# Two attention heads stacked per tile, and rotation tables made during an earlier feed-forward part and kept in DRAM

## The chip, the core and the metric

One core of one Trainium2 chip. The metric is the device time of one execution of the whole program in microseconds (us). The engines are TensorE (PE, with its weight loads PEld), VectorE (DVE), ScalarE (ACT), GpSimd (POOL), and SyncE (SP), which only issues transfers.

## What is computed

A stack of blocks over 256 tokens of width 1024, batch 1, all in float32. First two layers, each a gated feed-forward, a hybrid mixer and a second gated feed-forward, each with its norms; then a third block with a mixer of its own kind and a feed-forward:

```python
def first_block(x, ...):
    for l in range(DEPTH):          # DEPTH = 2
        f = swiglu(rms_norm(x, ffn1_pre_g[l]), ffn1_w_gu[l], ffn1_w_down[l])
        x = x + 0.5 * rms_norm(f, ffn1_post_g[l])
        m = hybrid_mixer(rms_norm(x, mix_pre_g[l]), ...)
        x = x + rms_norm(m, mix_post_g[l])
        f = swiglu(rms_norm(x, ffn2_pre_g[l]), ffn2_w_gu[l], ffn2_w_down[l])
        x = x + 0.5 * rms_norm(f, ffn2_post_g[l])
def second_block(x, ...):
    h = rms_norm_2(x, mix_norm_g[0])
    (u, c_b, c_c, c_x, q, k_c, v_c, k_s, v_s, k_w, v_w, nsa_gates, mix_gates) = split_projection(h @ w_in[0])
    y_ssm = s5_mixer(u, lam_re, lam_im, b_re, b_im, c_re, c_im, d, log_dt, w_glu)
    y_conv = short_conv_mixer(c_x, c_b, c_c, conv_w, conv_w_out)
    y_attn = nsa_mixer(q, k_c, v_c, k_s, v_s, k_w, v_w, nsa_gates, ...)
    ...                             # gates, w_out, then a last feed-forward
```

Two parts of the third mixer matter here. `s5_mixer` is a diagonal complex state-space recurrence, `lam_bar = exp(lam * exp(log_dt))`, for 32 groups of 64 states. `nsa_mixer` is attention with 8 query heads of width 64 on 2 key heads, with compressed, selected and window keys.

## The kernel before, in words

Every weight matrix is cut into chunks of 128 x 1024 float32 (512 KB), which SP streams into a ring of six slots `raw`. Each chunk is split in two: ACT rounds it to `whi` (`split_hi`, L465), DVE subtracts to get the rest `wlo` (`split_lo`, L472), and PE makes each product in three matmuls (L486 to L488, or L773 and L774 in the feed-forward). A slot is free for the split again once PE has consumed the chunk, so ACT and DVE run at most six chunks ahead of PE.

**The feed-forward** (`ffn_pe`, `ffn_act`, `ffn_dve`) has 22 hidden tiles. PE's order for tile j is gate(j), up(j), down(j-2); the last four down chunks come at the end (`held`) and need the hidden values of tiles 18 to 21. DVE's order for one tile is fixed in `tile`: sum the gate halves (L890), scale (L892), wait for the `wlo` split of one chunk (L472), sum the up halves (L895), multiply (L898), round (L902), subtract (L904), and split two more chunks. ACT's order is silu (L851), then three `whi` splits. The DVE split in the middle waits for the first of these three, which stands behind the silu, which waits for L892. Gate(j) needs the bank that tile j-2 has drained. In all layers tiles 2 to 5 and 18 to 21 are written out, the middle ones are a hardware loop.

**The third mixer** (`mix2_pe`, `mix2_act`, `mix2_dve`, `mix2_pool`) has an order written out by hand. Names are kept in the lists `BANKED2`, `JOBS2`, `BY_ACT2` and `BY_DVE2`, which give each product its PSUM bank and each wait its number. First come projections. Then q and k are transposed per head (L1480, L1487) into `qT` [64, 8, 256] and `kT` [64, 4, 256]; the compressed keys likewise (L1492), and the compressed scores are made per head (`cs0`, `cs1`, L1497). Then 16 rounds r, head h = r // 2 and token tile t = r % 2. PE's round is: scores of the two branches (L1509) with a mask added by a matmul (L1510), the state-space inputs `bu`, the transposes of the round before (L1548), one more streamed projection, values (L1574), and after each second round the state-space outputs (L1538). DVE takes the maximum of the scores (L2128), rotates the inputs by a cosine and sine table (L2137, L2138, L2143, L2144) and scans them (L2148); ACT makes the exponentials (L1823); POOL rotates back (L1918, L1919).

The scores of round r+1 use the same bank as those of round r, so PE waits there until ACT has read them, and ACT waits for DVE's maximum. The first maximum also stands behind DVE's work on `cs0` and `cs1` (L2076 to L2087), from which `pct` (L1556) is made.

The rotation tables have one [128, 2, 2, 256] piece per head, eight in all, made in two buffers (`table` and a part of `par`) one or two heads ahead: `turns` (ACT, L1661 and L1664), `fraction` (DVE, L1938 and L1939), `tables` (ACT, L1674 to L1679, sines, which need another function table of ACT than the exponentials). The coefficients `s5p` are made by small DVE operations on [128, 16] (L1979 to L1987 and L2033 to L2053), and POOL turns the output weights by them once `coef_ready` is set (L1901 to L1911).

Of the kernel before, what the change touches and what calls it, by code (L numbers as in the profile page):

```python
# [43 lines left out]
MIX2_CHUNKS = 90  # L44
HELD = 4
# [19 lines left out]
D_ROUNDS = D_MIXED + 16  # L65
CHANNELS = [f"cv{s}" for s in range(12)] + [f"e{j}" for j in range(len(EARLY))]
# [63 lines left out]
class Place:  # L130
# [17 lines left out]
    def later(self, rounds):  # L148
# [19 lines left out]
           "cv3", "hidt0", "hidt1", "cv4", "cmp0", "cmp1", "cv5", "qt00", "qt01", "qt10", "qt11", "kt0", "kt1", "cv6", "kct", "cs0", "cs1", "cv7"])  # L168
# [38 lines left out]
def block_program(nc, stream, x_in, pf_a, pf_b, pm, pm2, out):  # L207
    ctx = ExitStack()
    with ctx:
# [82 lines left out]
        qT = m1("qT", [HD, 8, S])  # L292
        kT = m1("kT", [HD, 4, S])
        blocks_scope = ExitStack()
        xchi, xclo = [blocks_scope.enter_context(nc.sbuf_tensor(name, [P, 2, 16, 16], F32R)) for name in ("xchi", "xclo")]
        blocks_scope.close()
        otok = m1("otok", [P, T, 512])
        hidT = m1("hidT", [P, 2, 16])
        kcn = m1("kcn", [16, HD])
        kcT = m1("kcT", [HD, 16])  # L300
# [10 lines left out]
        frac = m1("frac", [P, 2, S])  # L311
# [133 lines left out]
        consts2 = sem("consts2")  # L445

# [392 lines left out]
        def ffn_act(act, n, q, place, following):  # L839
# [25 lines left out]
            with act.Fori(0, 4) as i:  # L865
                for u in range(4):
                    j = 2 + u
                    tile(n * (FT - 2) + i * 4 + (u + 1), j, place.later(i * 2), range(3 * j + 3, 3 * j + 6))
            for j in range(18, FT - 1):
                tile(n * (FT - 2) + j - 1, j, place, range(3 * j + 3, 3 * j + 6))  # L870
            tile(n * (FT - 2) + FT - 2, FT - 1, place, [])
# [3 lines left out]
        def ffn_dve(dve, n, q, place, following):  # L875
# [41 lines left out]
            for j in range(2, 6):  # L917
                tile(n * FT + j, n * (FT - 2) + j - 2, j, place, gate_of(j), range(3 * j + 3, 3 * j + 6), free=down_of(j - 4) if j >= 4 else None)
            with dve.Fori(0, 3) as i:
                for u in range(4):  # L920
                    j = 6 + u
                    tile(n * FT + i * 4 + j, n * (FT - 2) + i * 4 + (j - 2), j, place.later(i * 2), gate_of(j), range(3 * j + 3, 3 * j + 6), free=down_of(j - 4))
            for j in range(18, FT):
                split = range(3 * j + 3, 3 * j + 6) if j < FT - 1 else []
                tile(n * FT + j, n * (FT - 2) + j - 2, j, place, gate_of(j), split, free=down_of(j - 4))
# [452 lines left out]
        def mix2_pe(pe, q, r, place, turns):  # L1378
# [95 lines left out]
            for t in range(T):  # L1474
                for b in range(2):
                    name = f"qt{t}{b}"
                    begin2(pe, name)
                    for a in range(4):
                        h = 4 * b + a
                        m = nc.tensor.transpose(bank2(name, slice(a * P, (a + 1) * P))[0:HD], xn[:, t, h * HD:(h + 1) * HD], ident[:, :])  # L1480
                    done(name, m)
            qn_ready.wait(pe, 2 * T)
            for t in range(T):
                name = f"kt{t}"
                begin2(pe, name)
                for a in range(4):
                    m = nc.tensor.transpose(bank2(name, slice(a * P, (a + 1) * P))[0:HD], xn[:, t, 512 + a * HD:512 + (a + 1) * HD], ident[:, :])  # L1487
                done(name, m)
# [1074 lines left out]
```

## Time and profile before

| | us |
|---|---|
| three runs | 1459.5, 1462.04, 1461.91 (median 1461.91) |
| the profiled execution | 1459.69 |
| its span in the trace | 1457.6 |
| PE busy | 1441.8 (99%) |
| DVE busy | 1145.0 (79%) |
| ACT busy | 766.8 (53%) |
| POOL busy | 143.6 (10%) |
| feed-forward two of layer two | about 773 to 950 |
| third mixer | about 951 to 1270, its rounds 1047 to 1167 |

The table reads as a kernel in which one engine is nearly always occupied. Busy PE time is modelled from the starts of pipelined matmuls, so 99% does not say that no time is lost there: a matmul at half clock is as busy as one at full clock. The granted clock has the mean 0.996.

### The profile page before, as it was taken

What the parts mean: (1) busy time and instruction counts of PE and PEld (TensorE: products, weight loads), DVE (VectorE), ACT (ScalarE), POOL (GpSimd) and SP (SyncE); (2) the same over time, 40 slices, a digit from 0 to 9 for tenths busy, and PEclk for the clock granted to TensorE, in tenths of its full rate; (3) what the DMA queues carried; (4) which work ended last, traced back from release to release, by engine and by line L of the source; (5) the groups of instructions that cost most, each with busy time, mean ns of one, the idle gap of its engine ahead of it and who ended that gap; (6) DMA issues with size and microseconds to landing.
All of it is one profiled execution on the core that took longest, in us unless ns stands there. A gap on an engine that the chain in (4) does not pass through costs nothing.

```text
span 1457.6 us, 24445 instructions
## 1 busy us (share of the span) xinstructions
PE 1441.8 (99%) x8561; PEld 1257.9 (86%) x8561; DVE 1145.0 (79%) x1831; ACT 766.8 (53%) x1253; POOL 143.6 (10%) x140
## 2 busy tenths in 40 slices
PE   8999999999999999999999999999999999999999
PEld 7888889888888888889988888888887899888887
DVE  5777777878787777777787787878899977577776
ACT  6343476663434543437656434478598665453432
POOL 0000015100000000002420000020433310000000
PEclk9999999999999999999999999999999999999999
DMA  8666555446656666565545656656422256546662
GB/s 321 194 200 200 195 165 176 163 149 193 201 190 199 209 201 201 195 193 168 166 159 181 203 188 201 195 182 210 151 87 83 85 179 189 175 160 197 196 200 84
DMA packets 71360, 261.74 MB, mean 180 GB/s; under 512 B 8048, under 2 KB 8048, under 8 KB 71024
## 3 DMA queue, kind: packets, MB, share of 16 engines
q1 hardware_dynamic: 69984, 253.79, 54.0%
q10 hardware_dynamic: 1296, 6.85, 1.3%
q8 instruction: 54, 0.88, 0.2%
q14 instruction: 26, 0.21, 0.0%
HBM read 259.56 MB, written 1.05 MB: 179 GB/s over the span
## 4 chain that ended last, share of the span: by engine, by line
PE 92%; DVE 4%; ACT 2%; issue 1%; POOL 0%; DMA 0%; ACTq 0%; DVEq 0%
PE work L773 25%; PE work L774 12%; PE acc L486 9%; PE acc L487 9%; PE acc L488 9%; PE work L486 8%; PE work L487 7%; PE work L488 7%; DVE wlo L472 1%; PE work L1509 1%; PE acc L1538 1%; ACT whi L465 1%; PE acc L1574 1%; PE work L1510 0%; PE work L678 0%
## 5 line engine op out<-in xcount | busy, mean ns | idle before, releaser
L472 DVE TENSOR_TENSOR wlo<-raw,whi 128x1024 fp32r<-128x1024 f32 (+1 forms) x460 | 549.9, 1222 | 174.8 <-ACT whi L465 173.4
L773 PE MATMUL work<-xboth,whi 128*128 128x512 f32 x1600 | 552.3, 391 | 0.0
L465 ACT ACTIVATE whi<-raw 128x1024 fp32r<-128x1024 f32 x480 | 475.2, 1039 | 59.6 <-PE work L488 33.5
L774 PE MATMUL work<-xboth,wlo 128*128 128x256 f32 x1600 | 442.2, 276 | 0.0
L773 PEld LDWEIGHTS work<-xboth,whi 128*128 128x128 f32 x1600 | 300.3, 188 | 64.3
L774 PEld LDWEIGHTS work<-xboth,wlo 128*128 128x128 f32 x1600 | 300.4, 188 | 3.7
L851 ACT ACTIVATE sg<-sg 128x256 f32<-128x256 f32 x100 | 41.8, 418 | 464.2 <-DVE sg L892 464.2
L486 PE MATMUL acc<-whi,hhi 128*128 128x512 f32 x440 | 173.2, 394 | 0.0
L487 PE MATMUL acc<-wlo,hhi 128*128 128x512 f32 x440 | 172.1, 391 | 0.0
L488 PE MATMUL acc<-whi,hlo 128*128 128x512 f32 x440 | 171.8, 390 | 0.0
L486 PE MATMUL work<-xboth,whi 128*128 128x256 f32 (+1 forms) x424 | 121.1, 286 | 0.0
L487 PE MATMUL work<-xboth,whi 128*128 128x256 f32 (+1 forms) x424 | 119.7, 282 | 0.0
L488 PE MATMUL work<-xboth,wlo 128*128 128x256 f32 (+1 forms) x424 | 119.3, 281 | 0.0
L488 PEld LDWEIGHTS acc<-whi,hlo 128*128 128x128 f32 x440 | 82.6, 188 | 19.1
L486 PEld LDWEIGHTS acc<-whi,hhi 128*128 128x128 f32 x440 | 82.5, 187 | 18.1
L487 PEld LDWEIGHTS acc<-wlo,hhi 128*128 128x128 f32 x440 | 82.6, 188 | 13.9
L486 PEld LDWEIGHTS work<-xboth,whi 128*128 128x128 f32 (+1 forms) x424 | 80.0, 189 | 0.7 <-issue 0.4
L487 PEld LDWEIGHTS work<-xboth,whi 128*128 128x128 f32 (+1 forms) x424 | 79.7, 188 | 0.2
L488 PEld LDWEIGHTS work<-xboth,wlo 128*128 128x128 f32 (+1 forms) x424 | 79.6, 188 | 0.1
L554 POOL TENSOR_TENSOR prstd<-pms,small 128x1 f32<-128x1 f32 x12 | 6.6, 551 | 730.8 <-DVE pms L562 730.8
L486 PE MATMUL work<-whi,xboth 128*128 128x512 f32 (+2 forms) x192 | 73.4, 382 | 2.6 <-DVE xboth L548 2.0
L487 PE MATMUL work<-wlo,xboth 128*128 128x512 f32 (+2 forms) x192 | 70.6, 367 | 0.0
(441 smaller groups left out, 2172.2 us busy)
## 6 DMA issues: line engine op xcount, KB each, us to landing
raw<-stream SPq DMA_DIRECT2D x480, 512.0 KB, 3.7
par<-pm ACTq DMA_DIRECT2D x2, 1644.5 KB, 7.1
pfa<-pf_a ACTq DMA_DIRECT2D x3, 516.0 KB, 4.7
pfb<-pf_b ACTq DMA_DIRECT2D x2, 516.0 KB, 8.1
x<-x_in SPq DMA_DIRECT2D x2, 512.0 KB, 5.8
out<-x SPq DMA_DIRECT2D x4, 256.0 KB, 2.0
par<-pm ACTq DMA_DIRECT2D x1, 820.0 KB, 4.2
pre<-pf_a ACTq DMA_DIRECT2D x1, 4.0 KB, 3.9
```

What stands on the lines that cost most here:

```text
L465: nc.scalar.activation(chunk(whi, place, c)[:, cols], chunk(raw, place, c)[:, cols], ACT.Copy).then_inc(hi_ready, 1)
L472: nc.vector.tensor_tensor(chunk(wlo, place, c)[:, cols], chunk(raw, place, c)[:, cols], chunk(whi, place, c)[:, cols].bitcast(F32), ALU.su ...
L486: return [nc.tensor.matmul(o, lhi, rhi, start=start, stop=False), nc.tensor.matmul(o, lhi, rlo, start=False, stop=False), nc.tensor.matmul ...
L487: nc.tensor.matmul(o, lhi, rlo, start=False, stop=False),
L488: nc.tensor.matmul(o, llo, rhi, start=False, stop=stop)]
L554: nc.gpsimd.tensor_tensor(prstd[:, t:t + 1], pms[:, t:t + 1], small[:, 0:1], ALU.pow).then_inc(prstd_ready, 1)
L773: nc.tensor.matmul(o[:, :], hi[:, k * P:(k + 1) * P], xboth[:, k, :], start=k == 0, stop=False)
L774: m = nc.tensor.matmul(o[:, 0:S], lo[:, k * P:(k + 1) * P], xhi[:, k, :], start=False, stop=k == KD - 1)
L851: nc.scalar.activation(sg[:, j % 2, :], sg[:, j % 2, :], ACT.Silu).then_inc(sg_ready, 1)
L1509: nc.tensor.matmul(bank2(f"sc{r}", slice(b * S, b * S + nkeys(t))), qT[:, h, t * P:(t + 1) * P], kT[:, 2 * b + h // 4, 0:nkeys(t)], start= ...
L1538: m = nc.tensor.matmul(acc[at:at + 32, 1, k % 2 * S:(k % 2 + 1) * S], left, rotated[:, r % 2, i // 2, i % 2, :], start=i == 0, stop=i == 3)
L1574: m = nc.tensor.matmul(acc[:, 0, at:at + HD], pT[:, r % 2, (b * 2 + k) * P:(b * 2 + k + 1) * P], xn[:, k, 768 + b * P + (h // 4) * HD:768 ...
```

## The change

Five things, which belong together.

1. **Stacked heads.** The columns of q, of its gates and the rows of the output weights are reordered on the host (`HEAD_ORDER`), so that a pair of neighbouring heads uses the two different key heads. q is transposed two heads at a time into `qT` [128, 4, 256]. `kT` becomes [128, 2, 2, 256], with one key head's rows filled and the rest zero. Scores contract over 128 rows instead of 64, and both branches are one matmul with up to 512 columns; the mask is one matmul too. The compressed keys are built the same way, and each `cs` is 4 matmuls of 16 columns instead of 8 of 8.
2. `cs1` now stands behind the streamed projection `cv7` in PE's order; before, it stood ahead of it.
3. **Coefficients and tables earlier.** `turns_act` and `turns_dve` are called once per tile, behind the tile's own work, in layer two's second feed-forward; for that feed-forward ACT and DVE have all tiles written out. All eight fractions are made there, and the sines and cosines of heads 2 to 7, which six transfers store to a DRAM tensor `spilled`. The cosines of heads 0 and 1 are finished in the mixer.
4. In the rounds ACT issues a load of the table of head h+1 (`load_turns`) in place of making it.
5. POOL makes the token counts and `magic` ahead of that feed-forward, clears `kT` and `kcT` ahead of the mixer, and turns the output weights as soon as all stores are done.

```diff
-            for t in range(T):
-                for b in range(2):
-                    name = f"qt{t}{b}"
...
-                        m = nc.tensor.transpose(bank2(name, slice(a * P, (a + 1) * P))[0:HD], xn[:, t, h * HD:(h + 1) * HD], ident[:, :])
...
+                for a in range(PAIRS):
+                    m = nc.tensor.transpose(bank2(name, slice(a * P, (a + 1) * P)), xn[:, t, a * P:(a + 1) * P], ident[:, :])
...
             evac2.wait(pe, BY_ACT2.index("kct") + 1)
             for t in range(T):
                 begin2(pe, f"cs{t}")
-                for h in range(8):
-                    m = nc.tensor.matmul(bank2(f"cs{t}", slice(h * 8, h * 8 + 8)), qT[:, h, t * P:(t + 1) * P], kcT[:, (h // 4) * 8:(h // 4) * 8 + 8], start=True, stop=True)
+                for a in range(PAIRS):
+                    m = nc.tensor.matmul(bank2(f"cs{t}", slice(a * 16, a * 16 + 16)), qT[:, a, t * P:(t + 1) * P], kcT[:, :], start=True, stop=True)
                 done(f"cs{t}", m)
-            channel(7)
+                if t == 0:
+                    channel(7)
...
-                for b in range(2):
-                    nc.tensor.matmul(bank2(f"sc{r}", slice(b * S, b * S + nkeys(t))), qT[:, h, t * P:(t + 1) * P], kT[:, 2 * b + h // 4, 0:nkeys(t)], start=True, stop=False)
-                    m = nc.tensor.matmul(bank2(f"sc{r}", slice(b * S + t * P, b * S + (t + 1) * P)), identr[:, :], maskr[:, :], start=False, stop=True)
+                both = bank2(f"sc{r}").rearrange("p (b n) -> p b n", b=2)
+                nc.tensor.matmul(both[:, :, 0:nkeys(t)], qT[:, h // 2, t * P:(t + 1) * P], kT[:, h % 2, :, 0:nkeys(t)], start=True, stop=False)
+                done(f"sc{r}", nc.tensor.matmul(both[:, :, t * P:(t + 1) * P], identr[:, :], maskr[:, :].unsqueeze(1).broadcast_to([P, 2, P]), start=False, stop=True))
...
+        def turns_act(act, j):
+            if j == 2:
...
+                s5a.inc(nc.scalar.activation(s5p[:, 0, :], par[:, PN["ldt"]], ACT.Exp))
...
+            if j % 2 == 1 and j < 19:
+                turn_counts(act, (j - 3) // 2)
+            elif j in (8, 12, 16, 20):
+                turn_sines(act, (j - 8) // 4)
+            elif j in (10, 14, 18):
+                k = (j - 10) // 4
+                turn_cosines(act, k)
+                tab.wait(act, 8 * k + 8)
+                for i in range(2):
+                    act.dma_start(spilled[TURN_ORDER[2 * k + i] - KEPT_TURNS], turn_stage(k, i).rearrange("p a b n -> p (a b n)")).then_inc(turns_stored, 16)
...
+        def turns_dve(dve, j):
...
+            elif j % 2 == 0 and j < 20:
+                n = (j - 4) // 2
+                part, g = turn_buffer(n // 2)[:, n % 2], TURN_ORDER[n]
+                tab_k.wait(dve, 4 * n + 4)
+                for i in range(2):
+                    vstep2.inc(stt(out=part[:, i, :], in0=tokens_f[:, :], scalar=s5p[:, 2, 2 * g + i:2 * g + i + 1], in1=part[:, i, :], op0=ALU.mult, op1=ALU.subtract))
+            elif 5 <= j < 20:
+                n = (j - 5) // 2
...
+                frac_ready.inc(ts(part, part, 0.5, -0.5, ALU.min, ALU.max))
+            if j == 9:
...
+                step(tt(sp(5), sp(5), sp(5), ALU.mult))
...
+            def load_turns(g):
...
+                rot_ready.wait(act, 2 * g - 2)
+                act.dma_start(table[g % 2].rearrange("p a b n -> p (a b n)"), spilled[g - KEPT_TURNS]).then_inc(turns_loaded[g % 2], 16)
...
-                if t == 0 and h + 1 < 8:
-                    tables(h + 1)
-                if t == 1 and h + 2 < 8:
-                    turns(h + 2)
+                if t == 0 and KEPT_TURNS <= h + 1 < 8:
+                    load_turns(h + 1)
...
-                if r % 2 == 1 and r < 12:
-                    fraction((r + 3) // 2)
```

At j = 2 DVE makes the nine operations on [128, 16] that stood at L1979 to L1987; the nineteen of L2033 to L2053 are spread in groups of three and four over tiles 9, 11, 13, 15, 17 and 19.

**DVE in layer two's second feed-forward, one middle tile.** Before:

```order
L890 TENSOR_REDUCE sg<-work0 128x256
L892 TENSOR_TENSOR sg<-sg,rrow 128x256
L472 TENSOR_TENSOR wlo<-raw,whi 128x1024
L895 TENSOR_REDUCE h32<-work1 128x256
L898 TENSOR_TENSOR h32<-sg,h32 128x256
L902 CAST hhi<-h32 128x256
L904 TENSOR_TENSOR hlo<-h32,hhi 128x256
L472 TENSOR_TENSOR wlo<-raw,whi 128x1024 x2
```

The end of tile 8 and all of tile 9 in the changed kernel (`pT` is here a buffer for a fraction):

```order
L476 TENSOR_TENSOR wlo<-raw,whi 128x1024 x2
L1735 SCALAR_TENSOR_TENSOR pT<-tokens_f,s5p,pT 128x256 x2
L897 TENSOR_REDUCE sg<-work0 128x256
L899 TENSOR_TENSOR sg<-sg,rrow 128x256
L476 TENSOR_TENSOR wlo<-raw,whi 128x1024
L902 TENSOR_REDUCE h32<-work1 128x256
L905 TENSOR_TENSOR h32<-sg,h32 128x256
L909 CAST hhi<-h32 128x256
L911 TENSOR_TENSOR hlo<-h32,hhi 128x256
L476 TENSOR_TENSOR wlo<-raw,whi 128x1024 x2
L1740 TENSOR_SCALAR pT<-pT 128x512
L1743 TENSOR_TENSOR s5p<-s5p 128x16
```

The tile itself is as it was; between two tiles there now stand two operations on [128, 256], or one on [128, 512] and up to four small ones.

**PE at the compressed scores and the first round's scores.** Before, with the 24 matmuls of `cv7` left out between the two pieces:

```order
L1492 MATMUL work2<-ident,kcn 64x16
L1497 MATMUL work3<-kcT,qT 128x8 x8
L1497 MATMUL work0<-kcT,qT 128x8 x8
```

```order
L1509 MATMUL work1<-kT,qT 128x128
L1510 MATMUL work1<-maskr,identr 128x128
L1509 MATMUL work1<-kT,qT 128x128
L1510 MATMUL work1<-maskr,identr 128x128
L486 MATMUL work2<-y5hi,whi 128x256
```

In the changed kernel, first ahead of `cv7`, then behind it:

```order
L1502 MATMUL work0<-ident,kcn 128x16
L1507 MATMUL work1<-kcT,qT 128x16 x4
```

```order
L1507 MATMUL work2<-kcT,qT 128x16 x4
L1520 MATMUL work3<-kT,qT 128x2x128
L1521 MATMUL work3<-maskr,identr 128x2x128
L490 MATMUL work0<-y5hi,whi 128x256
```

Half of the small matmuls are gone, two of the four score matmuls of a round, and `cs1` has moved from ahead of `cv7` to directly ahead of the first scores.

## Rows read from the trace of the kernel before

**Rows 1.** The page: busy time of PE, and the chain that ended last, by engine

```profile
PE 1441.8 (99%) x8561; PEld 1257.9 (86%) x8561; DVE 1145.0 (79%) x1831; ACT 766.8 (53%) x1253; POOL 143.6 (10%) x140
...
PE 92%; DVE 4%; ACT 2%; issue 1%; POOL 0%; DMA 0%; ACTq 0%; DVEq 0%
```

**Rows 2.** Waits of PE: line, whom for, us in total, times, longest

```profile
PE work L1509 <- ACT sm L1823: 1.5, 2, 1.2
...
PE work L1492 <- DVE kcn L2066: 0.6, 1, 0.6
```

**Rows 3.** DVE's timeline in the feed-forward: start us, duration us, line

```profile
850.62 0.69 DVE L890 TENSOR_REDUCE sg<-work 128x256 f32<-128x512 f32 x1
...
853.20 1.23 DVE L472 TENSOR_TENSOR wlo<-raw,whi 128x1024 fp32r<-128x1024 f32 x1 [1.43 <-ACT whi L465]
...
858.61 0.68 DVE L890 TENSOR_REDUCE sg<-work 128x256 f32<-128x512 f32 x1
```

**Rows 4.** PE's timeline there: the starts of two neighbouring down products

```profile
851.58 0.39 PE L486 MATMUL acc<-whi,hhi 128*128 128x512 f32 x1
...
859.80 0.39 PE L486 MATMUL acc<-whi,hhi 128*128 128x512 f32 x1
```

**Rows 5.** Timeline, DVE at tile 2 and tile 21, then PE in the held part

```profile
786.92 0.68 DVE L890 TENSOR_REDUCE sg<-work 128x256 f32<-128x512 f32 x1
...
939.25 0.68 DVE L890 TENSOR_REDUCE sg<-work 128x256 f32<-128x512 f32 x1
...
941.96 0.43 DVE L904 TENSOR_TENSOR hlo<-h,hhi 128x256 fp32r<-128x256 f32 x1
...
942.68 0.39 PE L486 MATMUL acc<-whi,hhi 128*128 128x512 f32 x1
```

**Rows 6.** DVE's timeline in the mixer: first and last small operation, and one fraction

```profile
982.88 0.18 DVE L1979 TENSOR_TENSOR s5p<-par,s5p 128x16 f32<-128x16 f32 x1 [0.37 <-ACT s5p L1710]
...
984.44 0.18 DVE L1987 TENSOR_SCALAR s5p<-s5p 128x16 f32<-128x16 f32 x1
...
990.36 1.00 DVE L1938 SCALAR_TENSOR_TENSOR frac<-tokens_f,s5p,frac 128x256 f32<-128x256 f32 x2
...
991.73 1.22 DVE L472 TENSOR_TENSOR wlo<-raw,whi 128x1024 fp32r<-128x1024 f32 x1
```

**Rows 7.** Groups of PE by line, 1020 to 1180: count, busy us, mean ns

```profile
L1497 PE MATMUL work<-kcT,qT 64*128 64x8 f32 x32 | 3.7, 253 | 0.3 <-ACT kcT L1652 0.3
...
L1480 PE MATMUL work<-ident,xn 128*64 128x128 f32 x16 | 1.9, 272 | 0.0
```

**Rows 8.** PE's timeline: a 512-column product, scores of a round with t = 0, with t = 1

```profile
1052.31 1.02 PE L1564 MATMUL acc<-sm,pcT 128*128 128x512 f32 x2
1053.16 1.02 PE L1564 MATMUL work<-sm,pcT 128*128 128x512 f32 x2
...
1060.40 0.48 PE L1509 MATMUL work<-kT,qT 64*128 64x128 f32 x2 [0.28 <-ACT sm L1823]
...
1061.65 0.33 PE L486 MATMUL work<-y5hi,whi 128*128 128x256 f32 x1
...
1068.01 0.70 PE L1509 MATMUL work<-kT,qT 64*128 64x256 f32 x2
...
1069.69 0.34 PE L486 MATMUL work<-y5hi,whi 128*128 128x256 f32 x1
```

**Rows 9.** Busy time by stretch; the first figure behind the engines is PE's granted clock

```profile
1041.00:1048.00 7.00, 7.00 (x44) 6.65 (x43) 5.77 (x24) 2.79 (x5) 0.63 (x1) 0.76 0.46 145
...
1103.00:1112.00 9.00, 8.19 (x39) 7.75 (x40) 8.83 (x14) 8.27 (x19) 2.52 (x2) 0.62 0.20 58
```

**Rows 10.** DVE's timeline: first and last operation on `cs1`

```profile
1045.21 0.22 DVE L2076 TENSOR_TENSOR ce<-work,cmask 128x64 f32<-128x64 f32 x1
...
1047.65 0.19 DVE L2087 TENSOR_TENSOR pc<-ce,cst 128x32 f32<-128x32 f32 x1
```

**Rows 11.** Groups of DVE by line in the rounds, 1049 to 1168

```profile
L1938 DVE SCALAR_TENSOR_TENSOR frac<-tokens_f,s5p,frac 128x256 f32<-128x256 f32 x12 | 9.7, 811 | 0.2
```

More of the change, by code:

```diff
@@ L44 @@
 MIX2_CHUNKS = 90
+PAIRS = 4
+HEAD_ORDER = [4 * (i % 2) + i // 2 for i in range(2 * PAIRS)]
 HELD = 4
@@ L445, in block_program @@
         consts2 = sem("consts2")
+        turns_stored, turns_loaded = sem("turns_stored"), [sem(f"turns_loaded{i}") for i in range(2)]
+        tokens_ready = sem("tokens_ready")
         block = ctx.enter_context(nc.Block())
@@ L837, in ffn_pe, with ffn_act @@
                  lambda m: pe.wait_ge(hlo_ready, n * FT + (BODY + m + 1)), turns)
-        def ffn_act(act, n, q, place, following):
+        def ffn_act(act, n, q, place, following, beside=None):
             def head(t):
@@ L864, in ffn_act @@
             split_hi(act, place, [7, 8])
[L865 to L869, printed above, removed]
+            if beside is None:
+                with act.Fori(0, 4) as i:
+                    for u in range(4):
+                        j = 2 + u
+                        tile(n * (FT - 2) + i * 4 + (u + 1), j, place.later(i * 2), range(3 * j + 3, 3 * j + 6))
+            for j in range(18 if beside is None else 2, FT - 1):
                 tile(n * (FT - 2) + j - 1, j, place, range(3 * j + 3, 3 * j + 6))
+                if beside is not None:
+                    beside(j)
             tile(n * (FT - 2) + FT - 2, FT - 1, place, [])
@@ L873, in ffn_act, with ffn_dve @@
                 split_hi(act, following, [0, 1])
-        def ffn_dve(dve, n, q, place, following):
+        def ffn_dve(dve, n, q, place, following, beside=None):
             def head(t):
@@ L916, in ffn_dve, with tiles @@
             dve.wait_ge(row_copied, n + 1)
[L917 to L925, printed above, removed]
+            def tiles(js):
+                for j in js:
+                    split = range(3 * j + 3, 3 * j + 6) if j < FT - 1 else []
+                    tile(n * FT + j, n * (FT - 2) + j - 2, j, place, gate_of(j), split, free=down_of(j - 4) if j >= 4 else None)
+                    if beside is not None:
+                        beside(j)
+            tiles(range(2, 6 if beside is None else FT))
+            if beside is None:
+                with dve.Fori(0, 3) as i:
+                    for u in range(4):
+                        j = 6 + u
+                        tile(n * FT + i * 4 + j, n * (FT - 2) + i * 4 + (j - 2), j, place.later(i * 2), gate_of(j), range(3 * j + 3, 3 * j + 6), free=down_of(j - 4))
+                tiles(range(18, FT))
             if following is not None:
@@ new lines, in turn_sines, with turn_cosines @@
+        def turn_sines(act, k):
+            if 0 < k < 3:
+                act.wait_ge(turns_stored, 32 * k)
+            frac_ready.wait(act, 2 * k + 2)
+            for scale, part in ((TWO_PI, 1), (TWO_PI / 2, 0)):
+                for i in range(2):
+                    tab.inc(nc.scalar.activation(turn_stage(k, i)[:, :, part, :], turn_buffer(k)[:, i], ACT.Sin, scale=scale))
+        def turn_cosines(act, k):
+            tab.wait(act, 8 * k + 4)
+            for i in range(2):
+                o = turn_stage(k, i)[:, :, 0, :]
+                tab.inc(nc.scalar.activation(o, o, ACT.Square))
+            tab.wait(act, 8 * k + 6)
+            for i in range(2):
+                o = turn_stage(k, i)[:, :, 0, :]
+                tab.inc(nc.scalar.activation(o, o, ACT.Identity, scale=-2.0, bias=1.0))
```

249 lines of the change are left out of this document (132 added, 117 removed).

## The prediction

> **What bounds the kernel now.** I read the page first, then the waits of PE, then timelines of the two places that the change touches. The page [rows 1] has PE busy for 1441.8 us, 99% of the span, and at the head of the chain with 92%. The list of PE's waits is short [rows 2]: 1.5 us behind ACT's exponentials and 0.6 us behind the compressed keys in the third mixer. So work taken from DVE, ACT or POOL gives time only where PE waits for it or where its clock has fallen, and work added to them costs time only once their lead over PE is used up. The change lightens them in the mixer and loads them in layer two's second feed-forward, so the question is how large the lead is in the second place.
>
> There the timeline of DVE holds a trap. DVE is idle for 1.43 us in each tile [rows 3], but that idle time isn't free: DVE scales the gate, ACT does its silu and then the split for which DVE waits, all in one line. From one L890 to the next this loop takes 7.99 us (850.62 to 858.61). PE needs 8.22 us for a tile (851.58 to 859.80) [rows 4]. The loop of DVE and ACT is thus only 0.23 us per tile faster than PE. DVE starts late (786.92 at tile 2) and catches up by this little, until it comes to the last tile at 939.25 [rows 5]. Nineteen periods of 7.99 us would bring it there at 938.7, so over the whole part it has 0.5 us to spare. Its last low half, started at 941.96 and 0.43 us long, is done at 942.39, and PE reads the last held hidden tile from 942.68: 0.3 us more. All the room that work added to DVE's loop can use up by the end of this feed-forward is 0.8 us.
>
> In the mixer PE loses time in a way that no wait shows: the granted clock. It has the mean 0.76 from 1041 to 1048 and 0.62 from 1103 to 1112 [rows 9], that is, stretches at the lower level of 1.2 GHz in place of 2.4. The first follows the 0.6 us wait and the 8-column matmuls of the compressed scores, the second the 1.2 us wait for ACT.
>
> **The change, part by part.** *DVE in the feed-forward.* Added are nine small dependent operations at tile 2; they stood in the mixer from 982.88 to 984.62, 1.7 us [rows 6]. Added are eight fractions. One took 1.37 us in the mixer, from 990.36 to the next split at 991.73 [rows 6], with waits of its own between its steps. These are now split over two tiles and the waits are gone; I take 1.2 us, together 9.6. Added are nineteen more small operations, 0.195 us apart (eight steps from 982.88 to 984.44), 3.7 us. The sum is 15.0 us. All of it stands between two tiles in DVE's order, behind the splits and ahead of the next L890, so it lengthens the loop, to about 8.8 us against PE's 8.22. ACT's 1.43 us doesn't shrink, since the silu can't begin before L892. Of the 15.0 us, 0.8 are covered, so PE's end of this part comes **14.2 us later**. The bounds are 15.6 (the fractions at 1.37 each) and nothing, if the waits of 1.43 us take the work up after all; I stay by the upper end, since the loop is serial in the rows.
>
> *ACT and POOL there.* ACT gets counts, sines, cosines and six store issues, behind its third split. It is 53% busy overall and comes to the silu well ahead of DVE, which in addition will be late; I cost it at nothing, and if that cover were gone it would add to the same loop. POOL has only idle time there. The six stores of 512 KB go out on ACT's queue while SP streams chunks that are needed two tiles later: nothing.
>
> *The clock at the end of the feed-forward.* When the last tiles come late, PE has only short pieces of work between waits in the last ten microseconds or so; in the held part it must wait several us for the hidden tile 21. Both stretches of low clock in the mixer follow shorter idling than this. They cost 1.7 us (7 us times 0.24) and 3.4 us (9 us times 0.38) [rows 9]. I add **2 us**, with 0 and 3.4 as bounds.
>
> *PE in the mixer.* The transposes of q: 16 took 1.9 us [rows 7], eight are left, 1.0 saved; those of k are eight of the same kind, four left, 0.5. The compressed scores: 3.7 us for 32 passes [rows 7], half saved, 1.8. The scores: a round with t = 0 takes 1.25 us (1060.40 to 1061.65) for two pairs over 128 columns, one with t = 1 takes 1.68 (1068.01 to 1069.69) for two pairs over 256 columns [rows 8]. So 128 columns cost 0.215 us and a pair of score and mask has 0.41 us on top. With one pair in place of two each round saves 0.41. A product over all 128 rows and 512 columns takes 0.85 us, though (1052.31 to 1053.16) [rows 8], with nothing on top; by it a round with t = 1 would save some 0.6. I take 0.5, in 16 rounds **8 us**, with 6.5 and 10 as bounds. Together 11.3 us.
>
> The weight of this term is where a rule speaks against the change. By the Trainium skill (TensorE: Matmul & The Clock Gate, Step-by-step: what each phase is for) the time to load weights goes by their columns, the number of rows K doesn't matter, and the streaming takes one cycle per column of the moving side. A round streams as many columns after the change as before. By that rule alone the stacking of two score products gives next to nothing; the rows show a fixed part, and I go by them.
>
> *Waits and clock in the mixer.* DVE loses some 8 us of work ahead of the compressed keys (1.7, two fractions at 1.37, and 3.7) and, in the rounds, the fractions, 9.7 us for L1938 alone [rows 11]; ACT loses the tables and their function table loads. The two waits of 0.6 and 1.5 us should go, 2.1, and with them the two stretches of low clock, 5.1. If they go only in part, DVE is what is late next: its scans and rotations stay, and POOL goes on beside it.
>
> *A new wait.* `cs1` now stands directly ahead of the first scores. From `cs1` DVE makes the compressed weights in 2.6 us (1045.21 to 1047.84) [rows 10]. Before, PE had `cv7` and two more products in between; now only the scores (0.84 us by the rows above) and the state inputs, six matmuls, which I estimate at as much again; then it waits for `pct`, some 1 us. The first maximum and the exponential come later too, so the compressed values wait again, by an estimate as long. I take **2.0 us**, between 0 and 3. The loads of the tables replace their making at the same place, behind the same wait for POOL, about two rounds ahead of use: nothing.
>
> **The sum.** Feed-forward +14.2 and +2; mixer -11.3, -2.1, -5.1 and +2.0. That is -0.3 us against the profiled execution, 1459.7: 1459.4. This execution lies 2.2 us under the median of the runs shown, so the median should come to **1461.6**. A measurement of this kernel can tell about 0.2% (2.9 us) from no change; the forecast is no change.
>
> **Rivals.** *The stacking of scores saves nothing* (the skill's rule above). The fixed 0.41 us per pair could belong to the change of operand between matmuls and stay. For it: the mask matmul still stands in each round, with twice the columns. Against: the difference between rounds of 128 and 256 columns. Then 8 us are missing, 1469.6, slower; it decides once a stacked round takes over 1.2 us on average.
>
> *The clock falls in the mixer all the same*, so the change doesn't recover what it should. The compressed scores are still tiny matmuls, and the new wait stands right behind them. Then 5.1 us are missing, 1466.7.
>
> *PE's clock stays up at the end of the feed-forward and the new wait isn't there*, because other work of DVE is early. Then 4 us better, 1457.6.
>
> *The feed-forward hides the added work.* For it: DVE is 79% busy over the span, and PE never waits there. Against it: the serial loop [rows 3, 4]. Then 16.2 us less, near 1445.5.
>
> **How the numbers follow.** Forecast 0.42, stacking without gain 0.18, clock falls again 0.14, clock stays up and no new wait 0.17, hidden 0.09. The first is the chance of no change, the second and third together slower, 0.32, the last two faster, 0.26. The range leaves out the hidden case and a little of the ends of the others: 1455.5 to 1470.
>
> **What would show it.** In the feed-forward of layer two the period from one L897 to the next (the old L890) should be near 8.8 us between tiles 4 and 19, PE should show waits there for DVE's `wlo` or hidden tiles of some 14 us in all, the longest at the held part, and the mixer should start about 14 to 16 us later. In the mixer the waits for the compressed keys and for the exponentials should be gone, a score product of a round with t = 1 with its mask should take 1.1 to 1.3 us, a wait of about 1 us should stand ahead of `pct`, and no clock under 1 should show in the rounds. From the start of the mixer to its end I expect some 16 us less than before. If the feed-forward is less than 5 us longer, the account of the serial loop is wrong and the kernel is clearly faster; if the mixer is less than 10 us shorter, it is slower.

## The result, and the profile after

| | before | changed kernel |
|---|---|---|
| median (all runs beside each other) | 1460.05 us | 1464.7 us (1463.29 to 1465.42) |
| ratio, 95% interval | | 1.0023 (1.0016 to 1.0031) |
| span of the profiled execution | 1457.6 us | 1462.6 us |
| granted clock | 0.996 | 0.998 |

The changed kernel is slower by a little over 0.2%, where the forecast was no change. Its 1464.7 us lie inside the range. The span grew by 5.0 us, where -0.3 was forecast.

The page of the changed kernel, the row of busy times and the chain by engine (they answer to [rows 1]):

```profile
PE 1432.4 (98%) x8485; PEld 1245.4 (85%) x8485; DVE 1148.2 (79%) x1832; ACT 751.6 (51%) x1242; POOL 143.1 (10%) x142
...
PE 80%; DVE 14%; ACT 3%; issue 2%; POOL 1%; DMA 0%; DVEq 0%; ACTq 0%
```

PE has 9.4 us less to do and still ends 5 us later. DVE had 4% of the chain and has 14%: it has become the bound in the second feed-forward and in the mixer. The waits of PE show it (line, whom for, us in total, times, longest; they answer to [rows 2]):

```profile
PE acc L490 <- DVE hlo L911: 3.3, 1, 3.3
PE work L490 <- DVE wlo L476: 2.5, 3, 1.2
...
PE acc L490 <- DVE wlo L476: 2.1, 2, 1.5
...
PE acc L1548 <- POOL rotated L2028: 1.7, 3, 0.9
PE work L1566 <- DVE pc L2157: 1.5, 1, 1.5
...
PE acc L697 <- DVE xn L612: 1.3, 1, 1.3
PE work L777 <- DVE h L905: 1.0, 1, 1.0
```

**The second feed-forward.** DVE's timeline there, starts of the gate sum L897 (before: L890) and what stands between (they answer to [rows 3] and [rows 5]):

```profile
864.51 0.88 DVE L1735 SCALAR_TENSOR_TENSOR pT<-tokens_f,s5p,pT 128x256 f32<-128x256 f32 x2
865.30 0.69 DVE L897 TENSOR_REDUCE sg<-work 128x256 f32<-128x512 f32 x1
...
867.88 1.23 DVE L476 TENSOR_TENSOR wlo<-raw,whi 128x1024 fp32r<-128x1024 f32 x1 [1.43 <-ACT whi L469]
...
874.25 0.69 DVE L897 TENSOR_REDUCE sg<-work 128x256 f32<-128x512 f32 x1
...
953.26 0.69 DVE L897 TENSOR_REDUCE sg<-work 128x256 f32<-128x512 f32 x1
```

The loop takes 8.95 us here (865.30 to 874.25), and the idle 1.43 us in it are as long as before: the added work stands in front of them and doesn't fill them. The last gate sum starts at 953.26 in place of 939.25, 14.0 us later. Near the end of this part the clock falls (stretch and its length, busy us of PE, PEld, DVE, ACT and POOL, then PE's granted clock, the share of the DMA engines and GB/s; all rows of stretches below read like this):

```profile
955.00:962.00 7.00, 5.46 (x13) 4.33 (x14) 4.64 (x9) 3.13 (x6) 0.22 (x1) 0.51 0.66 237
```

PE's first product of the mixer comes at 966.66 in place of 950.31, **16.35 us later**; 16.2 were forecast.

**The mixer.** From there to its end it is 11.3 us shorter than before, where 16.5 were forecast. A score product of a round with t = 1 and one with t = 0, on PE's timeline, each up to the state inputs (they answer to [rows 8]):

```profile
1069.36 1.02 PE L1520 MATMUL work<-kT,qT 128*128 128x512 f32 x2
1069.82 0.68 PE L1521 MATMUL work<-maskr,identr 128*128 128x256 f32 x1
1070.34 0.28 PE L490 MATMUL work<-y5hi,whi 128*128 128x256 f32 x1
...
1074.12 0.59 PE L1520 MATMUL work<-kT,qT 128*128 128x256 f32 x2
1074.36 0.47 PE L1521 MATMUL work<-maskr,identr 128*128 128x256 f32 x1
1074.66 0.28 PE L490 MATMUL work<-y5hi,whi 128*128 128x256 f32 x1
```

That is 0.98 us in place of 1.68, and 0.54 in place of 1.25. The later rounds take 1.08 and 0.61. From the score product of round 13 to that of round 15, where PE waits for nothing in either kernel, it needs 12.61 us (1148.79 to 1161.40) in place of 14.04 (1142.53 to 1156.57). So a round saves 0.715 us, 11.4 us in 16 rounds, more than the 8 forecast, and the stacking isn't what fell short. The low clock is gone from the mixer too: it is 1.00 from 1036 to 1069 and from 1069 to 1161, against [rows 9]. What is new stands in two groups. First, DVE in the busiest 100 us of the rounds, before and after:

```profile
1060.00:1160.00 100.00, 98.52 (x719) 82.90 (x718) 95.66 (x158) 79.26 (x159) 35.49 (x28) 0.97 0.29 90
```

```profile
1080.00:1180.00 100.00, 96.24 (x761) 82.98 (x760) 98.11 (x152) 46.76 (x106) 37.41 (x28) 1.00 0.42 133
```

DVE is busier than before, though the fractions ([rows 11] and their clamps, 2.6 us more) have left. Second, the seventeen low halves of the weights that DVE makes in the same rounds (1054 to 1156.5 before, 1069.3 to 1161.3 after; busy us, then mean ns of one):

```profile
L472 DVE TENSOR_TENSOR wlo<-raw,whi 128x1024 fp32r<-128x1024 f32 x17 | 21.9, 1305 | 0.0
```

```profile
L476 DVE TENSOR_TENSOR wlo<-raw,whi 128x1024 fp32r<-128x1024 f32 x17 | 26.8, 1591 | 0.0
```

They cost 4.9 us more for the same work. The same holds ahead of the rounds: four low halves of `u` (L2106) take 5.1 us there, 1.4 before (L2016), beside POOL's products of the coefficients, which now run from 1022 to 1036.

### The profile page after: what moved, and what is told of

The parts are those of the page before. It is cut to its first block, busy times and chain, and to the rows that moved or that the text cites. A ratio compares the mean times of both kernels' runs of the same rounds, so it can differ in the third digit from the quotient of the medians.

```text
span 1462.6 us, 24184 instructions
## 1 busy us (share of the span) xinstructions
PE 1432.4 (98%) x8485; PEld 1245.4 (85%) x8485; DVE 1148.2 (79%) x1832; ACT 751.6 (51%) x1242; POOL 143.1 (10%) x142
## 4 chain that ended last, share of the span: by engine, by line
PE 80%; DVE 14%; ACT 3%; issue 2%; POOL 1%; DMA 0%; DVEq 0%; ACTq 0%
PE work L777 21%; PE work L778 10%; PE acc L490 8%; PE work L490 7%; PE acc L491 7%; PE acc L492 7%; PE work L491 7%; PE work L492 7%; DVE wlo L476 6%; ACT whi L469 2%; DVE h L902 1%; PE acc L1548 1%; DVE sg L897 1%; DVE h L905 1%; DVE hlo L911 1%
## 5 line engine op out<-in xcount | busy, mean ns | idle before, releaser
L476 DVE TENSOR_TENSOR wlo<-raw,whi 128x1024 fp32r<-128x1024 f32 (+1 forms) x460 | 556.1, 1235 | 179.4 <-ACT whi L469 178.0
```

The source lines that it names most:

```text
L476: nc.vector.tensor_tensor(chunk(wlo, place, c)[:, cols], chunk(raw, place, c)[:, cols], chunk(whi, place, c)[:, cols].bitcast(F32), ALU.su ...
```

## The experiments

Each was timed beside the kernel before, whose median was 1459.86 us beside e1 to e4, 1461.9 beside e5 to e8, 1461.64 beside e9 to e11 and 1461.7 beside e12. So the ratios are what is to be compared. Spans carry a scatter of their own: in the changed kernel, e4, e7, e8 and e12, whose programs are the same up to the mixer, it starts between 966.34 and 967.56. The length of the mixer alone, from its first product to that of the next feed-forward, is free of this; it is 333.6 us before and 322.3 in the changed kernel.

**e1 and e2: each part alone.** In e1 the kernel before got only the stacked heads:

```diff
-                for b in range(2):
-                    nc.tensor.matmul(... qT[:, h, ...], kT[:, 2 * b + h // 4, 0:nkeys(t)], start=True, stop=False)
...
+                nc.tensor.matmul(both[:, :, 0:nkeys(t)], qT[:, h // 2, ...], kT[:, h % 2, :, 0:nkeys(t)], start=True, stop=False)
```

> The kernel before with the stacked heads alone (q, k, compressed keys, scores); tables and coefficients stay in the mixer, cs1 stays ahead of cv7. Theory: the stacking is what pays, and it pays without the moved tables. From the trace of the changed kernel PE has 0.62 us less in each of 16 score products (9.9), 1.75 less in the transposes and 1.95 less in the compressed scores, 13.6 in all; some 3 of it are lost again to waits for DVE and POOL, so 10 to 11 us faster than before, near 1450, with the second feed-forward unchanged. Rival: PE's time in the mixer can only be taken out once DVE and ACT are relieved of the tables; then the waits grow by what PE saves and it is faster by 5 us or less, 1455 or more.

Measured: 1458.49 us, ratio 0.9991 (0.9982 to 1.0). The theory falls and the rival stands, by more than it said: some 13 us less work for PE gave 1.3 us, which the interval hardly tells from none. Waits of PE in e1 and three stretches of its rounds:

```profile
PE work L1507 <- ACT sm L1826: 4.1, 4, 1.8
PE work L1490 <- DVE kcn L2070: 3.1, 1, 3.1
```

```profile
1080.00:1100.00 20.00, 17.73 (x138) 14.39 (x137) 19.57 (x35) 16.70 (x32) 5.42 (x5) 1.00 0.30 99
1100.00:1120.00 20.00, 17.48 (x127) 15.49 (x126) 19.62 (x30) 16.55 (x34) 7.20 (x6) 0.91 0.27 87
1120.00:1140.00 20.00, 18.28 (x133) 15.97 (x133) 19.52 (x33) 16.07 (x35) 7.63 (x6) 0.91 0.27 80
```

DVE is busy for 19.6 of 20 us while PE stands still for 2. The two waits of [rows 2] have grown from 2.1 to 7.2 us. In e2 the tables were moved, but the heads stayed single:

```diff
-        qT = m1("qT", [P, PAIRS, S])
-        kT = m1("kT", [P, 2, 2, S])
+        qT = m1("qT", [P, 8, S])
+        kT = m1("kT", [HD, 4, S])
```

> The changed kernel without the stacked heads: coefficients and tables in the second feed-forward and DRAM, one head per product as before, cs1 ahead of cv7. Theory: +16.3 us up to the start of the third mixer as in the changed kernel (DVE's serial loop, and the clock), and in the mixer only the two waits (2.1) and the two stretches of low clock (5.1) are won, so 9 to 12 us slower than before, near 1470. Rival: the moved work is worth more in the mixer (PE's faster pace there rests on it), then at most 5 us slower than before and the stacked heads alone gain little.

Measured: 1471.18 us, ratio 1.0085 (1.0072 to 1.0099), 12.4 us slower by the ratio and 11.5 by the spans, at the upper end of what the theory said. The moved tables alone win 4 us in the mixer for 15 lost in the feed-forward. In the rounds of e2 everything that the moved work was to give back does come back, since DVE has room beside the slower single heads:

```profile
1070.00:1168.00 98.00, 98.00 (x736) 82.01 (x734) 90.37 (x146) 42.07 (x104) 35.84 (x28) 1.00 0.38 123
```

PE never stands still and its clock is full. From the second score product to the last it needs 97.4 us in place of 102.4.

**e3 and e5: the same work, in DVE's idle time.** e3 put DVE's pieces one place too late:

```diff
                 nc.vector.tensor_reduce(h32[:, j % 2, :], both_halves(up), AX.X, ALU.add).then_inc(usum_ready, 1)
+                if beside is not None and j > 2:
+                    beside(j - 1)
```

> The changed kernel with DVE's added pieces of the second feed-forward put inside the next tile, between the sum of the up columns and the wait for ACT's silu, where the trace shows DVE idle for 1.4 us in each tile. Work and its order are the same. Theory: the added work costs time because it stands ahead of the next gate sum in a serial loop; in the idle time it costs nothing as long as a piece stays under 1.4 us. The period of the gate sum should go back from 8.86 to 8.2 us, the mixer start 13 to 16 us earlier, time 1448 to 1452. Rival: what slows the part is the amount of work (DVE's, or ACT's counts and sines ahead of its silu, or the six stores); then the time falls by less than 4 us, 1461 or more.

Measured: 1461.03 us, ratio 1.0008 (0.9999 to 1.0017). The expectation had misread the tile. Behind the sum of the up columns the silu has long been done; the 1.43 us of idle time stand ahead of the first low half and were still there, and the period only fell to 8.66. e5 put them where the trace has the idle time:

```diff
                 nc.vector.tensor_tensor(sg[:, j % 2, :], sg[:, j % 2, :], rrow[:, :], ALU.mult).then_inc(gr_ready, 1)
+                if beside is not None and j > 2:
+                    beside(j - 1)
                 split_lo(dve, at, split[:1])
...
-                    if beside is not None:
-                        beside(j)
```

> The changed kernel again with DVE's added pieces inside the next tile, now behind the scaling of the gate and ahead of the first low half. That is where DVE really is idle for 1.43 us (it waits for ACT's silu and the split behind it); the run before put them one place too late, where DVE wasn't idle, and the period only fell from 8.86 to 8.66. Theory: a piece takes 0.45 to 1.0 us, less than 1.43, so the loop is back at 7.99 us, PE sets the period at 8.22, the held part begins near 942 and the mixer some 14 to 16 us earlier than in the changed kernel: 1449 to 1452. Rival: with the pieces there ACT's own added work (counts, sines) or the stores set the pace, the period stays over 8.5 and the time over 1457.

Measured: 1448.29 us, ratio **0.9915** (0.9902 to 0.9929), as the theory said. DVE's timeline of one tile of e5:

```profile
859.07 0.68 DVE L897 TENSOR_REDUCE sg<-work 128x256 f32<-128x512 f32 x1
859.79 0.42 DVE L899 TENSOR_TENSOR sg<-sg,rrow 128x256 f32<-128x256 f32 x1
860.13 0.88 DVE L1735 SCALAR_TENSOR_TENSOR pT<-tokens_f,s5p,pT 128x256 f32<-128x256 f32 x2
861.65 1.23 DVE L476 TENSOR_TENSOR wlo<-raw,whi 128x1024 fp32r<-128x1024 f32 x1 [0.64 <-ACT whi L469]
...
867.05 0.68 DVE L897 TENSOR_REDUCE sg<-work 128x256 f32<-128x512 f32 x1
```

The fractions take 0.8 us out of the 1.43, and the loop is back at 7.98 us. The mixer starts 0.3 us later than before instead of 16.35. ACT's counts, sines and six stores are all still there, so they cost 0.3 us at most.

**e4: the order of `cs1` and `cv7`.**

```diff
-                if t == 0:
-                    channel(7)
+            channel(7)
```

> The changed kernel with the second compressed-score product back ahead of the channel product cv7, the order of before. Theory: the wait of 1.5 us for the compressed weights and a part of the one for pct's copy come from this order; they go and it is 1 to 2.3 us faster than the changed kernel. Rival: DVE is late there for other reasons (cs0 and cs1 share its chain), the time doesn't change (within 0.5 us).

Measured: 1464.67 us, ratio 1.004 (1.0026 to 1.0053). The interval overlaps that of the changed kernel, and the two spans are 1462.2 and 1462.6. The rival stands: the wait ahead of `pct` is 1.4 us in place of 1.5. The forecast had the wait right but not its cause; what else makes DVE late there wasn't tried. In e2, with single heads and this order, PE's list shows no wait there.

**e6: POOL's work moved.** Zeroing of `kT` and `kcT` moved into the feed-forward, the nine operations of the coefficients between POOL's two norms:

```diff
+            nc.gpsimd.memset(kT[:, :, :, :], 0.0).then_inc(consts2, 1)
+            nc.gpsimd.memset(kcT[:, :], 0.0).then_inc(consts2, 1)
...
             mean_pow(rstds[:, :, 0:8], means[:, :, 0:8], 8)
-            s5m.wait(pool, 2)
-            mean_pow(rstds[:, :, 8:12], means[:, :, 8:12], 4)
             pool.wait_ge(turns_stored, 96)
...
             wc_ready.inc(nc.gpsimd.tensor_copy(cre, a3))
+            s5m.wait(pool, 2)
+            mean_pow(rstds[:, :, 8:12], means[:, :, 8:12], 4)
```

> The changed kernel with POOL's work alone moved: the zeroing of kT and kcT to the second feed-forward, and the nine operations of the coefficients' products from behind the second norm (1022 to 1036) to between the two norms, near 993 to 1007, where DVE waits for ACT anyway. Theory: DVE's low halves of u (5.1 us for four, 1.4 before) and the weights' low halves beside them (up to 2.1 us each, 1.22 alone) were slow because POOL worked beside them, and that delayed PE at 974 (1.25 us) and at 1037 (1.45 us); both waits go, 2 to 2.7 us faster than the changed kernel. Rival: the time lost at 1037 is made good again by the wait for the compressed weights or by DVE in the rounds behind it, so that at most 1 us is won.

Measured: 1461.84 us, ratio 1.0006 (0.9997 to 1.0015), against 1.0023: 2.5 us by the ratios, 3.0 by the spans. The low halves of `u` in e6 (1015 to 1045):

```profile
L2108 DVE TENSOR_TENSOR y5lo<-u,y5hi 128x256 fp32r<-128x256 f32 x4 | 1.4, 420 | 0.0
```

They take 1.4 us again in place of 5.1, and PE's wait at 1037 is gone; that at the mixer's entry is 0.4 in place of 1.3.

**e7, e8, e12: what bounds the rounds.** e7 adds work to DVE, e8 takes some away:

```diff
+                if r % 2 == 1 and r < 12:
+                    for _ in range(2):
+                        step(tt(xclo[:, :], xchi[:, :].bitcast(F32), xchi[:, :].bitcast(F32), ALU.subtract))
```

> The changed kernel with two operations of DVE over 128x512 (0.69 us each) added to each of the rounds 1, 3, 5, 7, 9 and 11, where the fractions stood before: 8.6 us more work on DVE with the steps between, its result unused. Theory: with stacked heads DVE, not PE, sets the pace of the rounds (19.5 of 20 us busy in each stretch from 1080 to 1180 while PE waits), so 5 to 8 us are added. Rival: PE still bounds the rounds and DVE has slack there as in the kernel before; under 2.5 us are added.

Measured: 1472.92 us, ratio 1.0081 (1.0067 to 1.0095); the span is 9.0 us over that of the changed kernel and its mixer 8.7 us longer, a little more than the theory said. The added operations and the seventeen low halves in e7's rounds (1069.6 to 1170.4):

```profile
L2234 DVE TENSOR_TENSOR xclo<-xchi 128x512 fp32r<-128x512 f32 x12 | 13.7, 1143 | 0.2
L476 DVE TENSOR_TENSOR wlo<-raw,whi 128x1024 fp32r<-128x1024 f32 x17 | 22.2, 1323 | 0.2
```

The twelve operations cost 13.7 us in place of the 8.6 expected: the first of each pair takes 1.56 to 1.62 us beside POOL, the second 0.69. And the low halves, which now start later, are back at 1323 ns, as in the kernel before with its fractions. DVE's work grew by 8.3 us net, the rounds by 8.7. So each microsecond that DVE gets there costs about one; a part comes through PE's clock, which fell to a mean of 0.96 in the stretch shown below.

```diff
-                step(tt(scale, scale, ngate[:, :]..., ALU.mult))
-                step(tt(sg[:, :, :]..., acc[:, 0, ...]..., bc(scale..., HD), ALU.mult))
...
-                step(tt(four[:, :, :, 0, :], four[:, :, :, 0, :], four[:, :, :, 1, :], ALU.add))
```

> The changed kernel without three of DVE's operations in combining a pair of heads (the scales by the gates, the scaling of the values, the sum of the two branches; its output thus lacks the softmax's division, the gates and one branch): 2.6 us less for DVE in each of three rounds, 7.8 in all, nothing less for PE. Theory (DVE sets the pace of the rounds): 3 to 5 us faster than the changed kernel, until PE is the bound again. Rival (PE bounds, its waits come from single late signals elsewhere): under 1 us.

Measured: 1460.58 us, ratio 0.9996 (0.9987 to 1.0005), 3.9 us under the changed kernel by the ratios, its mixer 4.0 us shorter. Taking away 7.8 us pays for about half of it, so then PE is the bound again. PE, PEld and DVE in the stretch 1080 to 1160 of the changed kernel, of e7 and of e8:

```profile
1080.00:1160.00 80.00, 76.89 (x604) 66.23 (x604) 78.62 (x122) 35.85 (x88) 30.45 (x24) 1.00 0.44 139
```

```profile
1080.00:1160.00 80.00, 71.38 (x529) 60.35 (x530) 78.31 (x122) 30.71 (x74) 25.36 (x21) 0.96 0.40 125
```

```profile
1080.00:1160.00 80.00, 78.75 (x621) 67.57 (x622) 78.72 (x123) 36.43 (x88) 31.57 (x26) 1.00 0.45 142
```

DVE is equally full in all three; PE follows it. Where does DVE's work come from, if the fractions are gone? e12 halves POOL's work beside it:

```diff
-                tt(rotated[:, r % 2, 1, :, :], g2[:, :, :], sinr, ALU.mult)
                 rot_ready.inc(tt(rotated[:, r % 2, 0, :, :], g2[:, :, :], cosr, ALU.mult))
```

> The changed kernel with POOL making only half of each rotation in the rounds (the product with the sines is left out, so the states' output is wrong): POOL's work there falls from 35.5 us to about half, and nothing of DVE's or PE's instructions changes. In the changed kernel the 17 low halves in the rounds take 26.8 us (1591 ns each), in the kernel before the same 17 take 21.9 (1305), since the fractions then filled the time beside POOL. Theory: DVE's operations are slow where POOL works beside them; the mean of a low half falls to 1.3 us or less and the rounds, bounded by DVE, get 3 to 5 us shorter; up to 1.7 us of it can come from PE's waits for the rotation itself. Rival: the low halves are slow for another reason (what they read or when DMA writes it); their mean stays over 1.5 and only the 1.7 us of waits for POOL go.

Measured: 1459.28 us, ratio 0.9987 (0.9978 to 0.9996), 5.3 us under the changed kernel by the ratios, its mixer 5.4 us shorter. The same low halves of e12, and its stretch 1080 to 1160:

```profile
L476 DVE TENSOR_TENSOR wlo<-raw,whi 128x1024 fp32r<-128x1024 f32 x17 | 20.4, 1217 | 0.0
```

```profile
1080.00:1160.00 80.00, 79.94 (x631) 68.53 (x630) 77.58 (x132) 35.93 (x89) 16.74 (x13) 1.00 0.45 145
```

Nothing of DVE's instructions was touched, and 6.4 us of its time are gone: 1217 ns each in place of 1591. PE is full again, and from the second score product to the end of the mixer its lead over the kernel before grows by 15.7 us instead of 10.2. Up to 1.7 us of this can be PE's own waits for the rotation.

**e9, e10, e11: what the parts are worth together.**

> The changed kernel with both edits that paid: DVE's pieces in the time of the silu, and POOL's zeroing and coefficient products moved. Theory: the two places are apart, so the gains add: 1448.3 less 2.5 to 3, near 1445.5, or 14 to 15 us faster than before. Rival: the gain of POOL's move is swallowed by DVE in the rounds once nothing else is late, 1447.5 or more.

Measured: 1445.89 us, ratio 0.9897 (0.9882 to 0.9912): the gains of e5 and e6 add, and its edit is that of the two. e10 has `combine` behind `front` with a buffer of its own:

```diff
+        joined = m1("joined", [P, 2, S])
...
+                if r + 1 < ROUNDS:
+                    front(r + 1)
                 if r % 4 == 2 and r > 2:
                     combine(r // 4 - 1)
-                if r + 1 < ROUNDS:
-                    front(r + 1)
```

> The run before it with one more edit: DVE's combining of a pair of heads moved behind the maximum and the rotation of the next round, with a buffer of its own. One operation of it on 128x8 takes 1.05 us in three rounds and 0.17 in the last, where POOL is idle, so it seems to suffer from POOL's rotation that starts at the same moment; and the maximum behind it, for which ACT and then PE wait, comes 3.2 us late in those rounds. Theory: 1 to 2.5 us faster than the run before it. Rival: DVE's whole work sets the pace and only its order changes, within 0.5 us.

Measured: 1444.02 us, ratio **0.9886** (0.9871 to 0.9901), the best version of this study. It takes 1.9 us off e9, though by the two intervals alone they can't be told apart; their runs don't overlap (1443.84 to 1444.9 against 1445.74 to 1446.18). The operation on 128x8 takes about 168 ns in all four places. The first operation of the same step, also on 128x8, takes 256 to 429 ns in three of them, 146 in e9; in the fourth it takes 1252, as it did in e9. So most of the delay beside POOL is gone from the three: DVE has 1.7 us less to do from the second score product to the last, and the mixer is 1.6 us shorter. What is gone from PE's list is its waits for ACT's exponentials (0.9 and 0.5 us in e9), which fits the earlier maximum. The runs don't part the two causes.

e11 is e2 with the edit of e5.

> The kernel with moved tables but single heads (run e2), with DVE's pieces in the time of the silu. Theory: the second feed-forward costs nothing then, so 15 to 16 us less than e2's 1471.2, near 1455.5, 4 to 5 us faster than before. The four kernels before, stacked alone (1.4 us faster), tables alone with the free placing, and both (about 12 faster) then show that the two parts need each other: the stacking is worth 7 us with the tables gone and 1.4 without, since DVE bounds the rounds. Rival: the parts just add, then this kernel must be 10 to 11 us faster than before, near 1449.5.

Measured: 1457.17 us, ratio 0.9974 (0.9965 to 0.9984). The parts don't add: stacking alone 0.9991, tables alone 0.9974, both 0.9915. That is 1.3, 3.8 and 12.4 us; the stacked heads are worth 8.6 us once the tables have left the rounds.

## Why the prediction was wrong

*The second feed-forward* was right: 14.2 forecast, 14.0 measured at the last gate sum, and with the clock 16.35 against 16.2. PE's list has 6.9 us of waits there, not the 14 given as a sign, the longest at the held part as said; the rest of its delay stands in matmuls counted as busy, whose ends are modelled and of which some ran at half clock. The serial loop is shown by e5, which keeps all the work, puts it two instructions later and wins 15.4 us of span. The prediction listed among its bounds that the waits of 1.43 us take the work up; they can, but only where they stand.

*PE's own savings* were forecast at 11.3. The scores gave 11.4 in place of 8; the transposes of q (1.0 us left of 1.9) and the compressed scores (2.0 left of 3.7) gave what was said. The rival that stacking saves nothing is out. By the rule behind it (the Trainium skill, TensorE: Matmul & The Clock Gate, Step-by-step: what each phase is for) a round would take as long as before; the rows show 0.7 us less, more than the 0.41 that the prediction found as the fixed part of a pair. The prediction's own reckoning doesn't hold for the stacked pair either: from 0.54 us for twice 128 columns to 0.98 for twice 256, it has 0.10 us on top of its columns and not 0.41. One pair in place of two would by itself have saved 0.41. The rest came with the change from 64 rows to 128, or with the keys read in two pieces; no run takes these apart. That this term gave 3.4 us more than forecast is luck for the total, which would else have been missed by 8.7.

**The step that failed** is "Waits and clock in the mixer". It booked 7.2 us of waits and low clock as won because DVE loses the fractions, on top of all that PE saves by the stacking, and named what is late next ("its scans and rotations stay, and POOL goes on beside it") without a price. By itself the term holds: in e2, where the heads stay single, the old waits and the low clock go, and the rounds are 5.1 us shorter from the second score product to the last, against 4.9 booked for them there. On top of the stacking it doesn't fit under DVE. Two things were missing.

The first is that DVE had no room in the rounds. The row of the kernel before, shown above, has it at 95.7 of 100 us beside PE's 98.5. A change that shortens PE's rounds by a tenth makes DVE the bound, unless DVE loses as much. It does lose 12.3 us, but not net: POOL's rotation starts as soon as DVE's scan is done, and what DVE does next runs beside it. Before, the fractions took part of that time (one pair took 1.85 us there and 1.02 away from it), and some low halves came after. Now the low halves stand in it and give back 4.9 us. e7 shows the same from the other side: with other operations in the fractions' place the low halves are fast again. From the second score product on, 10.7 us for the scores (15 times 0.715) and 4.9 for the old waits and the clock should have come, 15.6; 10.2 came. e12 takes the delay away and gets 15.7.

The second is the sentence on POOL, "only idle time there". It holds for the feed-forward, but the change also lets POOL's coefficient products start some 20 us earlier in the mixer (1022 in place of 1026, in a mixer that itself starts 16 us later), onto DVE's low halves of `u`, and adds a zeroing of 128x1024 at the entry. The prediction sets no timeline of POOL beside DVE's. It cost 3 us of span by e6.

The new wait was forecast at 2.0 us from 0 to 3; between the first and the second score product the changed kernel loses 1.6 us with 0.7 saved in it, thus 2.3. So the mixer fell short by 5.4 us in the rounds, 2.9 ahead of them (5.6 were booked up to the first score product, 2.7 are there) and 0.3 in the new wait, less 3.4 that the scores gave more: 5.2 of the 5.3 us by which the span was missed.

## What to carry to other kernels

Idle time of an engine in a serial loop can be used only by work that stands exactly where the engine waits; the same instructions two places earlier cost their full length (e5 against the changed kernel: 15.4 us of span), and two places later most of it (e3: 11.7 us of span over e5). Before taking work from the bounding engine, read the next engine's busy share in the same stretch: at 96% its gain is capped, and what is cut there must be cut with it. When work leaves an engine, ask what slides into its place and beside which neighbour: for DVE and POOL a removed operation may only have kept another one out of the slow time.

## What the runs showed of the hardware

An operation of DVE with two operands in SBUF waits until POOL's product beside it is through. The smallest shows it best, one of POOL's products and DVE's operation on 128x8 in the changed kernel:

```profile
1109.11 1.29 POOL L2027 TENSOR_TENSOR rotated<-g,par 128x512 f32<-128x512 f32 x1 [3.14 <-PE work L1521]
1109.37 1.06 DVE L2180 TENSOR_TENSOR rs<-rs,ngate 128x8 f32<-128x8 f32 x1
```

POOL's ends at 1110.40, DVE's at 1110.42; in two later rounds they end at 1137.09 and 1137.11, 1163.78 and 1163.81. Where POOL was idle the same operation took 0.17 us, a sixth. The low halves of 128x1024 took 1211 to 2149 ns in the changed kernel's rounds and 1212 to 1226 in e12. Operations that read work tiles of PSUM in the same rounds kept their time (0.68 us for 128x512 in all of these traces). The Trainium skill (SBUF - State Buffer, Who interferes with whom) says that the two engines share a port pair by an exclusive lock, and that an operation of DVE with two SBUF inputs contends with one of POOL that reads SBUF. These traces agree, for the low halves and for the 128x8 operation. Two operands aren't the whole rule: in e10 an operation on 128x8 with a single operand waited too, 256 to 1252 ns in place of 146, and ended 0.02 to 0.03 us behind POOL's each time.

One pair of score and mask products for both branches in place of two saves the same at either width: 0.71 us in the round of 128 columns and 0.70 in that of 256 shown above, 0.64 and 0.59 in the later rounds.
